# Variance of the convolution's layer norm: summed into four columns, root and reciprocal there, the row made by one product of diagonals

## What is computed

```
def layernorm(x, g, b):
    mu = jnp.mean(xf, axis=-1, keepdims=True)
    var = jnp.mean(jnp.square(xf - mu), axis=-1, keepdims=True)
    y = (xf - mu) * lax.rsqrt(var + EPS) * g + b

def conv_mixer(h, w_pw1, b_pw1, w_dw, b_dw, ln_g, ln_b, w_pw2, b_pw2):
    a = h @ w_pw1 + b_pw1
    u = a[..., :D_MODEL] * jax.nn.sigmoid(a[..., D_MODEL:])
    u = causal_depthwise_conv(u, w_dw) + b_dw
    u = jax.nn.silu(layernorm(u, ln_g, ln_b))
    return u @ w_pw2 + b_pw2
```

## Time and profile before

| | us |
|---|---|
| median of 3 runs (lowest, highest) | 1859.13 (1856.85, 1860.11) |
| the profiled execution | 1857.53 |
| its span in the trace | 1855.5 |
| TensorE busy in it | 1802.2 (97%) |
| VectorE, ScalarE, GpSimd busy | 806.4, 756.1, 780.8 |
| mean granted TensorE clock | 0.992 of full |

### The profile page before, as it was taken

The page is one execution under the profiler, slowest core; times in us unless marked ns, Lnnn a source line. Parts: engine busy times, 40 slices in busy tenths (PEclk is TensorE's granted clock), DMA queues, the critical chain, the costliest instruction groups (busy, mean ns, idle before and its releaser), DMA issues.

```text
span 1855.5 us, 20252 instructions
## 1 busy us (share of the span) xinstructions
PE 1802.2 (97%) x7952; PEld 1442.4 (78%) x7952; DVE 806.4 (43%) x1358; ACT 756.1 (41%) x1200; POOL 780.8 (42%) x360
## 2 busy tenths in 40 slices
PE   7999989999999999989999999999999999999987
PEld 6887768888888777478888888877877888668866
DVE  3794442210121189842210220187868832336563
ACT  4523345321342356444321342346555332444542
POOL 3343224444444459824444444443635543433211
PEclk9999999999999999999999999999999999999989
DMA  5232112332323233012333233333323322322101
GB/s 188 80 102 69 58 43 87 98 102 91 102 91 102 80 102 103 1 57 91 95 98 99 94 91 102 97 108 91 103 74 97 105 99 68 110 70 79 58 23 46
DMA packets 100094, 160.31 MB, mean 86 GB/s; under 512 B 7296, under 2 KB 30208, under 8 KB 100000
## 3 DMA queue, kind: packets, MB, share of 16 engines
q1 hardware_dynamic: 100000, 159.02, 27.8%
HBM read 156.90 MB, written 2.10 MB: 86 GB/s over the span
## 4 chain that ended last, share of the span: by engine, by line
PE 90%; DVE 5%; ACT 2%; issue 2%; DMA 0%; POOL 0%; SPq 0%; POOLq 0%; DVEq 0%; ACTq 0%
PE bank L585 27%; PE bank L586 27%; PE bank L587 27%; PE bank L834 2%; PE bank L877 1%; PE bank L665 1%; PE bank L997 1%; ACT prob L1247 1%; PE bank L768 1%; PE bank L1016 0%; DVE rg_u L2008 0%; PE bank L750 0%; PE bank L973 0%; PE bank L850 0%; DVE rg_u L2005 0%
## 5 line engine op out<-in xcount | busy, mean ns | idle before, releaser
L2354 POOL TENSOR_TENSOR w_lo<-w_raw,w_hi 128x1024 fp32r<-128x1024 f32 (+1 forms) x286 | 693.6, 2429 | 1025.2 <-ACT w_hi L1124 1025.2
L1124 ACT ACTIVATE w_hi<-w_raw 128x1024 fp32r<-128x1024 f32 (+1 forms) x286 | 300.6, 1054 | 584.2 <-PE bank L587 579.0
L585 PE MATMUL bank<-x_hi,w_hi 128*128 128x512 f32 (+1 forms) x1264 | 505.6, 400 | 2.1 <-DVE x_lo L1678 1.3
L587 PE MATMUL bank<-x_hi,w_lo 128*128 128x512 f32 (+1 forms) x1264 | 493.7, 391 | 0.0
L586 PE MATMUL bank<-x_lo,w_hi 128*128 128x512 f32 (+1 forms) x1264 | 493.3, 390 | 0.0
L585 PEld LDWEIGHTS bank<-x_hi,w_hi 128*128 128x128 f32 (+1 forms) x1264 | 237.2, 188 | 60.7 <-issue 11.7
L586 PEld LDWEIGHTS bank<-x_lo,w_hi 128*128 128x128 f32 (+1 forms) x1264 | 237.3, 188 | 54.0 <-issue 5.1
L587 PEld LDWEIGHTS bank<-x_hi,w_lo 128*128 128x128 f32 (+1 forms) x1264 | 237.1, 188 | 51.6
L585 PE MATMUL bank<-w_hi,f_hi 128*128 128x512 f32 x512 | 200.0, 391 | 0.0
L587 PE MATMUL bank<-w_hi,f_lo 128*128 128x512 f32 x512 | 199.3, 389 | 0.0
L586 PE MATMUL bank<-w_lo,f_hi 128*128 128x512 f32 x512 | 199.2, 389 | 0.0
(11 more groups left out here) (283 smaller groups left out, 2106.8 us busy)
## 6 DMA issues: line engine op xcount, KB each, us to landing
w_raw<-in_mlp_w SPq DMA_DIRECT2D x128, 512.0 KB, 3.7
w_raw<-in_even_w_in SPq DMA_DIRECT2D x48, 512.0 KB, 3.8
w_raw<-in_dsa_w_in SPq DMA_DIRECT2D x28, 512.0 KB, 3.6
w_raw<-in_odd_w_in SPq DMA_DIRECT2D x24, 512.0 KB, 3.6
w_raw<-in_conv_w_pw SPq DMA_DIRECT2D x32, 256.0 KB, 3.0
w_raw<-in_even_w_out SPq DMA_DIRECT2D x16, 512.0 KB, 3.8
w_raw<-in_dsa_w_out SPq DMA_DIRECT2D x8, 512.0 KB, 3.7
w_raw<-in_conv_w_pw SPq DMA_DIRECT2D x8, 512.0 KB, 3.8
```

What stands on the lines that cost most here:

```text
L585: e.matmul(o, sh, mh, start=first, stop=False)
L587: m = e.matmul(o, sl, mh, start=False, stop=last)
L1124: e.activation(hi, src, ACT.Copy).then_inc(*w_hi.up(u))
L2354: e.tensor_tensor(lo, src, hi.bitcast(F32), ALU.subtract).then_inc(*w_lo.up(u))
```

## The change

The squares become the stationary operand, 128 x 128 for each tile of tokens, and the moving one is a 128 x 4 block of `pick`: tile t's block has 1/1024 in column t and zero in the others. So each square gives four products with 4 columns, all added up in bank 1, columns 0 to 3, and the variance stands with tokens on the partitions, 128 x 4. Root and reciprocal work on these four columns (`stat(2, 7)`), four diagonals times 1024 go to `spare`, and one product with `mean_ones` writes the row of factors to bank 2, where the normalisation reads it. `pick` is made by five memsets at the start of the program, and the two reciprocals of 256 columns are gone. A reserve in the memory plan shrinks by the 16 columns that `pick` takes.

```diff
+        pick = sb("tile_picks", [P, T, T])
-        sb("place_of_stages", [P, 88])
+        sb("place_of_stages", [P, 72])
...
+        picks_made = signal("picks_made", ["made"])
-        row_diag = signal("row_diagonals", [0, 1, 2, 4])
-        row_mm = signal("row_product", [0, 1, 2, 4])
+        row_diag = signal("row_diagonals", [0, 1, "ln", 2, 4])
+        row_mm = signal("row_product", [0, 1, "ln", 2, 4])
...
             empty(VAR_BANK)
+            w.wait_ge(*picks_made.last())
             for n, k in enumerate(MEAN_ORDER):
+
                 w.wait_ge(*cent_sq.at(k))
-                m = e.matmul(bank[VAR_BANK][:, :], mean_ones, csq[n % 2][:, :], start=n == 0, stop=n == KD - 1)
+                for t in range(T):
+                    m = e.matmul(bank[VAR_BANK][:, 0:T], csq[n % 2][:, t * P:(t + 1) * P], pick[:, t, :],
+                                 start=n == 0 and t == 0, stop=n == KD - 1 and t == T - 1)
                 m.then_inc(*(mean_mm.up("var") if n == KD - 1 else sq_used.up(k)))
+            w.wait_ge(*row_diag.at("ln"))
+            e.matmul(bank[ROOT_BANK][:, :], mean_ones, flat_spare, start=True, stop=True).then_inc(*row_mm.up("ln"))
...
             w.wait_ge(*mean_mm.at("var"))
-            e.activation(bank[ROOT_BANK][:, :], bank[VAR_BANK][:, :], ACT.Sqrt, bias=epsc[:, 0:1]).then_inc(*var_root.up("root"))
+            e.activation(stat(2, 7), bank[VAR_BANK][:, 0:T], ACT.Sqrt, bias=epsc[:, 0:1]).then_inc(*var_root.up("root"))
...
+            w.wait_ge(*own_dve.after(e.memset(pick[:, :, :], 0.0)))
+            for t in range(T):
+                m = e.memset(pick[:, t, t:t + 1], 1.0 / D)
+            m.then_inc(*picks_made.up("made"))
...
-            w.wait_ge(*own_dve.after(e.reciprocal(RSTD[:, conv_part(0)], RSTD[:, conv_part(0)])))
+            w.wait_ge(*own_dve.after(e.reciprocal(stat(2, 7), stat(2, 7))))
+            for t in range(T):
+                m = e.tensor_scalar(spare[:, t, :], ident, stat(2, 7, t), float(D), ALU.mult, ALU.mult)
+            m.then_inc(*row_diag.up("ln"))
+            w.wait_ge(*row_mm.at("ln"))
             norm_part(0, 0)
-            w.wait_ge(*own_dve.after(e.reciprocal(RSTD[:, conv_part(1)], RSTD[:, conv_part(1)])))
             lo_part(0, 0)
```

## The result

| us | before | after |
|---|---|---|
| median of 11 runs (lowest, highest) | 1857.66 (1856.85, 1860.11) | 1863.20 (1859.92, 1864.55) |
| profiled execution, its span | 1857.53, 1855.5 | 1863.48, 1861.4 |
| mean granted clock in it | 0.992 | 0.988 |

What follows compares the result with a forecast made beforehand. TensorE was taken as the bound, 90% of the span, with a 5.24 us gap before pw2. Terms +0.1, +0.03 and -0.67 sum to -0.5 us, giving 1858.6 us from the runs' median; range 1856.2 to 1865.0.

Steps and rivals of the forecast that it cites:

- (a): Variance loop: 64 small products at the pace of their weight loads, +0.1 us, bounds -0.6 and +4.5.
- rival A: Clock falls inside the variance loop because 4-column products do not keep it up: +5.1 us, 1864.2; chance 0.30.
- (b): Last variance product to first normalisation: new root, reciprocal, diagonals and row product take 2.57 us, +0.03 us.
- rival D: Variance loop: weight loads do not hide behind such short products, +3.9 us, 1863.0; chance 0.05.
- (c): VectorE: second reciprocal goes without a successor, so the first low part starts earlier, -0.67 us.
- (d): Waits on VectorE and TensorE, and the five memsets at the start: new waits harmless, memsets cost nothing.
- (e): TensorE's restart in pw2: clock kept up only in part, same loss as now, 4.7 us at half rate, 2.3 lost.
- rival C: Row product in the gap saves the clock, TensorE restarts fast, supply limits the gain: -0.8 us, 1858.3; chance 0.12.
- slack of 0.3 us: End of pw2's first half: last low part ready 0.3 us before its products begin, capping a faster restart's gain.

Runs made afterwards that it cites:

- s128: Changed kernel with 128 moving columns, all but four unused, picks in the existing tile spare so addresses stay as before: 1858.29 us, ratio to before 1.0003.
- w128: Changed kernel with 128 moving columns, 124 of them zero, in a tile of their own; later tiles 224 bytes higher: 1870.24 us, ratio 1.0064.
- s4_ahead: s4 with two idle products of 512 columns filling the 1.5 us pause ahead of the variance loop: 1860.37 us, ratio to before 1.0014.
- s4: Changed kernel, still 4 columns, with picks in the existing tile spare, made by VectorE during the mean, no memsets at the start: 1862.92 us, ratio 1.0025.
- w64: Changed kernel with 64 moving columns, 60 of them zero, in a tile of their own; later tiles 32 bytes higher: 1874.81 us, ratio 1.009.
- w16: Changed kernel with 16 moving columns, twelve of them zero, in a tile of their own; later tiles 32 bytes higher: 1875.04 us, ratio 1.0089.
- wide_sum: Changed kernel with the variance summed as before, 8 products of 512 columns; new row kept, its values not the variance's: 1857.0 us, ratio to before 0.9996.
- no_second: Kernel before without the reciprocal for the second half of the tokens, which are then multiplied by the root: 1857.03 us, ratio 0.9995.
- before_warm: Kernel before with five idle products of 512 columns in TensorE's 5.2 us gap between variance and pw2: 1857.42 us, ratio 0.9999.
- s128_warm: s128 with three idle products of 512 columns in the two pauses around the row product: 1858.23 us, ratio 1.0001.
- s64: Changed kernel with 64 moving columns, picks in the existing tile spare so addresses stay as before: 1862.67 us, ratio to before 1.0017.

## Why the prediction was wrong, point by point

**The step that failed** is, in the sum, term (a): +0.1 us for the variance loop, which takes for granted that the clock stays at 2.4 GHz while only thin products run. It measured +4.69 us, with the granted clock at 0.50 from 1.6 us into the loop on, and the row product behind it, priced at 1.02 us in (b), took 2.07 for the same reason. The case was seen, as rival A; what failed is its weighing, a chance of 0.30 where four columns lost the clock in every traced run. I let two rows speak against it that hold 128-column products, and the earlier trace rows. They were right about their own width: s128 and w128 hold the clock. They said nothing on a width 32 times smaller, and the prediction itself noted that nothing in the trace is as thin. The stretch of the earlier trace rows is also short: its 18 products take 2.5 us, and in s4_ahead even four columns held the clock for 5.0 us before it fell. I had argued "loads and small products do count for something" from rows where the two came together; in the loop of after TensorE and its loads show as fully busy (1.00 and 1.00 from 785 to 786), no less than with 128 columns in s128 (7.00 and 6.77 in 7 us), and only the width of the products differs. The Trainium skill, "TensorE: Matmul & The Clock Gate" (PE-mode transpose), says that transposes do not count as busy for the clock as matmuls do. A matmul with almost nothing moving behaved so here. The 128-column transposes of the earlier trace rows did not: they ran at 421 ns and then, with only transposes before, at 273, and there the measurement decides.

**Its price** was right and its road was not quite. Named were +4.8 for six squares at half rate, +0.85 for the row product and -0.5 for the rest, +5.1 in all; measured were +4.69, +1.04 for the part to the normalisation (the row product alone 2.07 instead of the predicted 1.87) and -0.65, +5.08 in all. The squares at half clock followed each other every 1.71 us against the 1.74 expected. The start of the fall I had counted from the last product before the pause, 3.1 us on. That gave the right place, and it was partly luck: by the same count it was 3.1 us in s4, but 3.5 in w64, 4.5 in w16 and about 5 in s4_ahead. The measured 1863.20 lies inside the range only because the range took in a part of rival A. Two bounds do not come out of their own terms. Eight squares of 0.63 us are 2.6 us under 7.67, and become the -0.6 of (a) only with 0.25 us a square for a hand-over, which no row was named for; and three and a half squares in rival A give 2.8 + 0.85 - 0.5 = +3.15, not +2.6.

**(a)** +0.1 us, as long as the clock is full: near enough. The loop is 7.62 us with 64 and 7.84 with 128 columns, 7.67 before. No loop of four columns ran at full clock to its end; while it did in s4_ahead, two squares took 1.83 us (the squares of one buffer start at 784.99, 786.82 and 788.66), against 1.94 in s128 and 1.91 before, so four columns would come to about -0.3 us, an estimate from these rows. The width changes the pace little, 0.92 to 0.97 us a square from 4 to 128 columns, as the row with data as weights said, and rival D is out: at full clock the 64 loads of 0.19 us do hide.

**(b)** +0.03: nearly right. It is 2.64 us in wide_sum against the 2.57 worked out and 2.54 before. The row product took 1.12 or 1.13 us after its pause, not 1.02; the four diagonals 0.87 and 0.88, so the second multiply is free.

**(c)** -0.67: right where it was measured, -0.65 in after and -0.66 in no_second at TensorE's restart. In after the low part starts at 801.89, right behind the high part. At the end of pw2 0.4 us of it were left in no_second.

**(d)** Right: s4 has no memsets at the start and costs what after costs.

**(e)** The clock after the restart: I took the same loss as before. It fell at 794.9 in s128 and at 797.2 in wide_sum, with pauses of 1.48 and 2.08 us around the row product, and was back at 801.7 and 800.6: 5.3 and 3.4 us of pw2 at half clock, on either side of the 4.7 that I took. So the row product in the middle did not save the clock in any traced run, and rival C's first half is out. The Trainium skill, "TensorE: Matmul & The Clock Gate" (Why this matters for your kernels), asks for short gaps between bursts of matmuls; by it, as the prediction read it, both gaps would be harmless, and the traces do not agree. Rival C's second half, that the supply would take the gain away, is borne out by the traces: with the clock held by idle products the stage gains 0.0 us (before_warm) and 0.35 us (s128_warm against s128). The slack of 0.3 us of the earlier trace rows was the right thing to read.

So the forecast of no visible change would have been right for products of 128 columns (s128: 1.0003 [0.9994, 1.0011]), and the code as written was a case of its own.

## To carry to other kernels

Turning a product round so that little moves and much is loaded can cost half the clock although the engine looks busy without a break; read the granted clock in that very stretch, and if it falls, try it with 128 columns moving and most of them thrown away, which here cost 0.2 us of loop against 4.7. That only undid the loss: s128 is no faster than the kernel before. A row about another width is no evidence on this one: where the trace has no row of the same shape, the rival stays open, and rows of other shapes should not lower its chance. And before paying for a restart at full clock, look whether the supply could have fed it.

## What the runs showed of the hardware, unexpected

- Granted clock against width, with 128-column loads between all products and TensorE 1.00 busy: 4 and 16 columns fell to 1.2 GHz within the loop; 64 fell in w64, stayed up in the traced run of s64, and by the times went either way in one program (1857 against 1863 us); 128 stayed at 2.4 GHz. With a pause of 1.5 us ahead the fall came 1.5 to 3.0 us into the loop, without it 5.0 us, in one trace. Whether the columns moved or the zeros among them matter was not told apart: the added columns are zeros, and they held the clock nevertheless.
- The clock fell around the row product although TensorE was never idle for more than 2.1 us: at 794.9 in s128, in the pause of 2.08 us behind it, and in wide_sum at 797.2, when pw2 had been running again for 1.5 us.
- Tiles that lie 32 bytes higher made 1536 products 6 ns longer each and the program 0.7% slower. An experiment that adds a tile needs a control with nothing but the shift.
